# The gated-delta inverse: 16x16 diagonal blocks gathered one to a partition and solved by forward substitution

## What is computed

```python
G = jnp.cumsum(g, axis=-1)
decay = jnp.exp(jnp.where(incl, G[..., :, None] - G[..., None, :], -jnp.inf))
kb = k * beta[..., None]
L = jnp.where(strict, jnp.einsum('bhncd,bhnsd->bhncs', kb, k) * decay, 0.0)
rhs = jnp.concatenate([v * beta[..., None], kb * jnp.exp(G)[..., None]], axis=-1)
sol = lax.linalg.triangular_solve(L + jnp.eye(CHUNK), rhs, left_side=True, lower=True)
u, w = sol[..., :dv], sol[..., dv:]
# then, chunk after chunk:
v_new = u_c - w_c @ S;  o_c = q_c @ S + a_c @ v_new;  S = S * gl_c + k_c^T @ v_new
```

## Time and profile before

| | us |
|---|---|
| median of three runs | 2791.84 |
| the profiled execution, its time | 2790.25 |
| the profiled execution, its span | 2788.5 |
| TensorE busy | 2584.4 (93%) |
| VectorE busy | 1761.7 (63%) |
| ScalarE busy | 1150.0 (41%) |
| share of TensorE in the chain that ended last | 82% |
| share of VectorE and ScalarE in it | 9% and 5% |

### The profile page before, as it was taken

The page is one execution under the profiler, slowest core; times in us unless marked ns, Lnnn a source line. Parts: engine busy times, 40 slices in busy tenths (PEclk is TensorE's granted clock), DMA queues, the critical chain, the costliest instruction groups (busy, mean ns, idle before and its releaser), DMA issues.

```text
span 2788.5 us, 48740 instructions
## 1 busy us (share of the span) xinstructions
PE 2584.4 (93%) x17978; PEld 2278.9 (82%) x17978; DVE 1761.7 (63%) x2936; ACT 1150.0 (41%) x1720; POOL 73.7 (3%) x149
## 2 busy tenths in 40 slices
PE   6995789999998999988999999899999999889998
PEld 4873568885457899968889999799988999688998
DVE  1767574447964786765476676665557667654765
ACT  3333332220024544462354554644546446624544
POOL 0000000001100000000110000000000000000000
PEclk8997899999999999999999999999999999999999
DMA  7460033225752366530056551365524655300563
GB/s 262 166 196 1 28 116 106 90 88 184 242 192 83 121 196 192 178 113 1 24 170 189 178 181 61 116 186 180 167 92 136 195 181 159 128 1 27 177 187 131
DMA packets 104988, 377.96 MB, mean 136 GB/s; under 512 B 11671, under 2 KB 12695, under 8 KB 104352
## 3 DMA queue, kind: packets, MB, share of 16 engines
q1 hardware_dynamic: 91296, 327.58, 36.7%
q0 software_dynamic: 12528, 47.62, 5.2%
q10 hardware_dynamic: 1040, 1.05, 0.1%
HBM read 375.15 MB, written 1.05 MB: 135 GB/s over the span
## 4 chain that ended last, share of the span: by engine, by line
PE 82%; DVE 9%; ACT 5%; issue 2%; DMA 1%; POOL 0%; DVEq 0%; ACTq 0%; SPq 0%; POOLq 0%
PE gb L474 19%; PE gb L475 19%; PE gb L476 19%; PE gb L588 5%; PE gb L1439 2%; DVE w_lo L433 2%; PE mb L1457 2%; PE gb L1455 2%; PE gb L521 1%; PE gb L523 1%; PE mb L1736 1%; PE gb L522 1%; PE mb L554 1%; PE gb L997 1%; PE gb L1717 1%
## 5 line engine op out<-in xcount | busy, mean ns | idle before, releaser
L474 PE MATMUL gb<-Xs,w_hi 128*128 128x256 f32 (+1 forms) x3552 | 1063.3, 299 | 25.7 <-DVE Xs L637 12.5
L475 PE MATMUL gb<-Xs,w_hi 128*128 128x256 f32 (+1 forms) x3552 | 1059.0, 298 | 0.0
L476 PE MATMUL gb<-Xs,w_lo 128*128 128x256 f32 (+1 forms) x3552 | 1058.8, 298 | 0.0
L427 ACT ACTIVATE w_hi<-raw 128x1024 fp32r<-128x1024 f32 x592 | 622.8, 1058 | 858.2 <-PE gb L476 786.8
L433 DVE TENSOR_TENSOR w_lo<-raw,w_hi 128x1024 fp32r<-128x1024 f32 x592 | 715.9, 1223 | 249.6 <-ACT w_hi L427 246.4
L474 PEld LDWEIGHTS gb<-Xs,w_hi 128*128 128x128 f32 x3552 | 672.1, 189 | 64.6 <-issue 23.2
L475 PEld LDWEIGHTS gb<-Xs,w_hi 128*128 128x128 f32 x3552 | 671.2, 189 | 27.9 <-issue 1.0
L476 PEld LDWEIGHTS gb<-Xs,w_lo 128*128 128x128 f32 x3552 | 670.8, 189 | 27.3
L476 PE MATMUL gb<-Fs,w_lo 128*128 128x256 f32 x880 | 243.8, 277 | 0.0
L474 PE MATMUL gb<-Fs,w_hi 128*128 128x256 f32 x880 | 243.8, 277 | 0.0
L475 PE MATMUL gb<-Fs,w_hi 128*128 128x256 f32 x880 | 243.8, 277 | 0.0
(11 more groups left out here) (334 smaller groups left out, 2939.3 us busy)
## 6 DMA issues: line engine op xcount, KB each, us to landing
raw<-in_up SPq DMA_DIRECT2D x264, 512.0 KB, 3.6
raw<-in_down SPq DMA_DIRECT2D x96, 512.0 KB, 3.6
R<-in_mod_later POOLq DMA_DIRECT2D x80, 512.0 KB, 4.0
raw<-in_gdn_in SPq DMA_DIRECT2D x64, 512.0 KB, 3.6
raw<-in_down SPq DMA_DIRECT2D x48, 384.0 KB, 4.0
raw<-in_hgrn_in SPq DMA_DIRECT2D x32, 512.0 KB, 4.1
raw<-in_ev_in SPq DMA_DIRECT2D x24, 512.0 KB, 4.5
raw<-in_gla_in SPq DMA_DIRECT2D x24, 512.0 KB, 4.0
```

The source lines that it names most:

```text
L427: nc.scalar.activation(w_hi[:, slot], raw[:, slot], ACT.Identity).then_inc(*hi_ready.inc())
L474: nc.tensor.matmul(to, w_hi[:, w_slot, k, :], x_hi, start=start, stop=False)
L475: nc.tensor.matmul(to, w_hi[:, w_slot, k, :], x_lo, start=False, stop=False)
L476: return nc.tensor.matmul(to, w_lo[:, w_slot, k, :], x_hi, start=False, stop=stop)
```

## The change

The first four of the seven levels (blocks up to 16) go. In their place the 128 diagonal blocks of 16x16 (8 blocks in each of 16 instances) are gathered one to a partition, inverted there, and put back:

- VectorE makes three small selection tables once, at the program's start (`dve_picks`).
- VectorE masks `low_T` to its diagonal blocks, four heads at a time, after heads 3 and 7 of the score loop.
- TensorE gathers: 16 products whose stationary operand is one column in 16 of the masked matrices, and whose moving operand is a 128x16 selection table. The result is 128 partitions x (16x16).
- VectorE solves: for row r = 1 to 15 one multiply of r x r elements and one sum over them, each waiting for the one before.
- Meanwhile TensorE transposes v and k as before, but ScalarE now scales all four tiles of a head, and TensorE's transposes wait for ScalarE alone.
- The 128 small inverses are spread out to full block rows by VectorE (one multiply of 2048 elements) and ScalarE (8 scaled copies of 256 elements), turned back by 16 transposes each, and copied by VectorE and ScalarE (four copies of 512 elements each) to `inv_T` and `inv`.
- The levels then run from level 4: 12 steps in place of 28.

```diff
@@ pe_gdn
+            act_a.due("pe")
+            pe.wait_ge(*mixed.due("pe", 4))
+            pe.wait_ge(*low_masked.due("pe", 2))
+            if i == 0:
+                pe.wait_ge(*picks_made.due("pe"))
+            for r in range(SUB):
+                last = nc.tensor.matmul(mb[:, 2, r * SUB:(r + 1) * SUB], sub_rows[:, :, r], pick_row[:, :], start=True, stop=True)
+            last.then_inc(*subs_out.inc())
             for h in range(HG):
...
                 if h >= 2:
-                    pe.wait_ge(*act_a.due("pe", 2 if h == 2 else 1))
-                    pe.wait_ge(*dve_a.due("pe"))
+                    pe.wait_ge(*tokens_kept.due("pe"))
...
+            pe.wait_ge(*tokens_kept.due("pe", 2))
+            pe.wait_ge(*spread_dve.due("pe"))
+            for r in range(SUB):
+                last = nc.tensor.transpose(score_banks[r // 4][:, (r % 4) * P:(r % 4 + 1) * P],
+                                           sub_rows_T[:, :, :, r].rearrange("p b c -> p (b c)"), ident[:, :])
+                if r % 4 == 3:
+                    last.then_inc(*inv_T_turned.inc())
+            pe.wait_ge(*spread_act.due("pe"))
+            for c in range(SUB):
+                last = nc.tensor.transpose(gb[:, c // 4, (c % 4) * P:(c % 4 + 1) * P],
+                                           sub_cols[:, c].rearrange("p b i -> p (b i)"), ident[:, :])
+                if c % 4 == 3:
+                    last.then_inc(*inv_turned.inc())
+            pe.wait_ge(*inv_made.due("pe", 4))
+            pe.wait_ge(*inv_T_made.due("pe", 4))
+            steps = [(l, g) for l in range(FIRST_LEVEL, LEVELS) for g in range(4)]
@@ act_gdn
+                nc.scalar.activation(k_dec[:, h, :], gb[:, 2 + h % 2, 0:P], ACT.Identity, scale=e_last[:, h:h + 1])
+                nc.scalar.activation(kb_g[:, h, :], gb[:, 2 + h % 2, P:2 * P], ACT.Identity, scale=beta_g[:, h:h + 1]).then_inc(*tokens_kept.inc())
+            act.wait_ge(*solved.due("act"))
+            for b in range(NSUB):
+                last = nc.scalar.activation(sub_cols[:, :, b, :], sub_inv, ACT.Identity, scale=pick_sub[:, b:b + 1])
+            last.then_inc(*spread_act.inc())
+            for g in range(4):
+                act.wait_ge(*inv_turned.due("act"))
+                nc.scalar.activation(X[:, :, T:2 * T].rearrange("p h (m c) -> p h m c", c=SUB)[:, :, :, 4 * g:4 * g + 4],
+                                     gb[:, g, :].rearrange("p (c h m) -> p h m c", c=4, h=HG), ACT.Identity).then_inc(*inv_made.inc())
@@ dve_gdn
+            nc.vector.memset(sub_inv, 0.0).then_inc(*dve_step.inc())
...
+            nc.vector.tensor_copy(Pflat[:, 10240:10496:SUB + 1], ones[:, 0:SUB]).then_inc(*dve_step.inc())
             for h in range(HG):
...
+                if h % 4 == 3:
+                    dve.wait_ge(*mixed.sent())
+                    quad = lambda z: z[:, h - 3:h + 1].rearrange("p h a t -> p (h a) t")
+                    nc.vector.tensor_tensor(quad(low_sub), quad(low_T), same_sub[:, :].unsqueeze(1).broadcast_to([P, 2 * 4, P]),
+                                            ALU.mult).then_inc(*low_masked.inc())
+            dve.wait_ge(*subs_out.due("dve"))
+            dve.wait_ge(*dve_step.sent())
+            low = mb[:, 2, 0:SUB * SUB].rearrange("p (i j) -> p i j", j=SUB)
+            for r in range(1, SUB):
+                terms = sub_prod[:, 0:r * r].rearrange("p (c j) -> p c j", j=r)
+                link(dve, nc.vector.tensor_tensor(terms, sub_inv[:, 0:r, 0:r], low[:, r:r + 1, 0:r].broadcast_to([P, r, r]), ALU.mult))
+                last = nc.vector.reduce_sum(sub_inv[:, 0:r, r], terms, AX_X)
+                if r < SUB - 1:
+                    link(dve, last)
+            last.then_inc(*solved.inc())
...
+            nc.vector.tensor_tensor(sub_rows_T.rearrange("p b c i -> p b (c i)"), flat.unsqueeze(1).broadcast_to([P, NSUB, SUB * SUB]),
+                                    pick_sub[:, :].unsqueeze(2).broadcast_to([P, NSUB, SUB * SUB]), ALU.mult).then_inc(*spread_dve.inc())
+            for g in range(4):
+                dve.wait_ge(*inv_T_turned.due("dve"))
+                nc.vector.tensor_copy(sub_rows[:, :, 4 * g:4 * g + 4], score_banks[g].rearrange("p (i m) -> p m i", i=4)).then_inc(*inv_T_made.inc())
```

More of the change, by code:

```diff
@@ L39 @@
 LEVELS = 7
+SUB = 16
+NSUB = P // SUB
+FIRST_LEVEL = 4
 MOD_TILES = 16
@@ L247, in build @@
         dve_a = signal("dve_a")
+        picks_made = signal("picks_made")
+        low_masked = signal("low_masked")
+        subs_out = signal("subs_out")
+        solved = signal("solved")
+        spread_dve = signal("spread_dve")
+        spread_act = signal("spread_act")
+        inv_turned = signal("inv_turned")
+        inv_T_turned = signal("inv_T_turned")
+        inv_made = signal("inv_made")
+        inv_T_made = signal("inv_T_made")
+        tokens_turned = signal("tokens_turned")
+        tokens_kept = signal("tokens_kept")
         inv_y = signal("inv_y")
@@ L1364, in build @@
         inv_T = inst(Pflat, 8192)
+        low_sub = inv_T
+        sub_rows = inv_T.rearrange("p h a (b i) -> p (h a b) i", i=SUB)
+        sub_inv = Pflat[:, 10240:10496].rearrange("p (c i) -> p c i", i=SUB)
+        sub_prod = Pflat[:, 10496:10752]
+        sub_rows_T = M[:, :, :].rearrange("p h t -> p (h t)").rearrange("p (b c i) -> p b c i", b=NSUB, i=SUB)
+        sub_cols = W[:, 0:4, :].rearrange("p a t -> p (a t)").rearrange("p (c b i) -> p c b i", b=NSUB, i=SUB)
         prod = [Pflat[:, 10240 + 512 * s:10752 + 512 * s] for s in range(2)]
@@ L1424, in pe_gdn @@
                         last = nc.tensor.transpose(gb[:, bank, t * P:(t + 1) * P], P2[:, c + h, t * P:(t + 1) * P], ident[:, :])
[L1425 to L1431, removed]
+                last.then_inc(*tokens_turned.inc())
+            pe.wait_ge(*tokens_kept.due("pe", 2))
[14 more added lines that the diff above has]
+            steps = [(l, g) for l in range(FIRST_LEVEL, LEVELS) for g in range(4)]
             def product(n):
                 l, g = steps[n]
-                if l:
+                if l > FIRST_LEVEL:
                     pe.wait_ge(*inv_done.due("pe"))
@@ L1539, in act_gdn @@
             pe_a.due("act")
+            act.wait_ge(*act_a.sent())
+            act.wait_ge(*mixed.due("act", HG))
             for h in range(HG):
-                act.wait_ge(*pe_a.due("act"))
-                if h == 0:
-                    act.wait_ge(*mixed.due("act", HG))
+                act.wait_ge(*tokens_turned.due("act"))
                 for t in range(TC):
-                    last = nc.scalar.activation(vb[:, h, t, :], gb[:, h % 2, t * P:(t + 1) * P], ACT.Identity, scale=beta[:, t, h:h + 1])
-                last.then_inc(*act_a.inc())
-            for n in range(4 * LEVELS):
+                    nc.scalar.activation(vb[:, h, t, :], gb[:, h % 2, t * P:(t + 1) * P], ACT.Identity, scale=beta[:, t, h:h + 1])
+                nc.scalar.activation(k_dec[:, h, :], gb[:, 2 + h % 2, 0:P], ACT.Identity, scale=e_last[:, h:h + 1])
[8 more added lines that the diff above has]
+                                     gb[:, g, :].rearrange("p (c h m) -> p h m c", c=4, h=HG), ACT.Identity).then_inc(*inv_made.inc())
+            for n in range(4 * (LEVELS - FIRST_LEVEL)):
                 act.wait_ge(*inv_y.due("act"))
@@ L1629, in dve_gdn @@
+            for l in range(FIRST_LEVEL, LEVELS):
                 for g in range(4):
-                    if l:
-                        dve.wait_ge(inv_done.sem, inv_base_dve[0] + 4 * (l - 1) + g + 1)
+                    if l > FIRST_LEVEL:
+                        dve.wait_ge(inv_done.sem, inv_base_dve[0] + 4 * (l - 1 - FIRST_LEVEL) + g + 1)
                     dve.wait_ge(*inv_z.due("dve"))
@@ L2060, in _ @@
                                     ALU.mult).then_inc(*lam_prod.inc())
+            dve_picks(dve)
             dve_mod(dve)
```

21 lines of the change are left out of this document (15 added, 6 removed).

## The result

| | us |
|---|---|
| changed kernel, median of four runs | 2761.51 (2760.56 to 2771.83) |
| kernel before, median of four runs | 2791.53 (2790.07 to 2804.28) |
| ratio after to before | 0.9891, interval 0.9854 to 0.9928 |
| forecast | 2731, range 2714 to 2756 |
| changed kernel, the profiled execution: time, span | 2762.44, 2760.4 |

The kernel became 30 us faster, half of what was forecast, and its time lies outside the range.

A forecast was written before the change was run, and what follows sets the result against it. The inverse was taken as bound by TensorE and on the path. Each mixer: 15.1 us added, 42.9 removed, 2.3 back at start-up, -30.1; both -60.2, from 2790.25 to 2730.0, so a 2731 us median, range 2714 to 2756.

The forecast's parts named there:

- What bounds the kernel, and the 16 steps removed: In each mixer's inverse, bound by TensorE and on the path: 16 steps at 2.68 us go, saving 42.9 us.
- Masks: VectorE's two masking multiplies after the scores: 2.64 us, net 2.2 after catching up; TensorE starts to gather at 2.3.
- Gather: TensorE's sixteen 16-column products before the solve: 3.5 to 6.6 us, taken as 3.5 from line 1386.
- upper bound of 6.6: TensorE's gathering products: 6.6 us if reading every 16th element costs 1.88 times, as in VectorE's masked copies.
- the first rival: Stride-16 stationary loads and copies reading PSUM across take 1.88 times: 5.6 us a mixer, 2742 us; chance 16 in 100.
- Solve, tokens, spreading: Between gathering and turning back: VectorE's solve 8.0 us, ScalarE's tokens 9.4, spreading 2.29 on VectorE and 3.3 on ScalarE.
- Turning back and start-up: Transposes before the levels, partly at low clock, end at 24.2 us; the levels' start-up then gives 2.3 us back.
- At nothing: Tables at program start, some 1.3 us in VectorE's idle time, and clearing with the diagonal, 0.4 us, cost nothing.
- the fourth rival: Gain returns as a wait for weights or the output projection's weight split: near 2790 us; chance 2 in 100.

## Why the prediction was wrong

By the changed kernel's trace, gdn0 and gdn1, step by step:

| step | forecast, us | gdn0 | gdn1 |
|---|---|---|---|
| last score multiply of before to the gather | 2.3 | 1.6 | 1.9 |
| gather to the solve | 3.7 | 7.1 | 7.1 |
| solve | 8.0 | 8.2 | 8.2 |
| solve's end to turning back | 2.5 | 2.5 | 2.5 |
| turning back to the first product of the levels | 7.7 | 6.4 | 7.3 |
| sum: start of the levels | 24.2 | 25.8 | 27.0 |
| levels | 30.0 | 29.9 | 30.2 |

The first row counts from where the last score multiply ended in the kernel before, 12.06 and 10.37 us behind the decay multiply. From the changed kernel's own last score multiply it is 1.4 us in both.

- *What bounds the kernel, and the 16 steps removed.* Right: the levels take 29.9 and 30.2 us with 12 steps.
- *Masks.* Right within a microsecond. VectorE caught up more than I gave it.
- *Gather.* The term was 3.5 us and the measurement is 7.1, above the upper bound of 6.6. I took line 1386 as the nearest row; the stride doubled it at the full clock, and the low clock would have doubled it as well. This second failed step cost 3.6 us in each mixer and was in part made up by the masks and the turning back. It is the mechanism of the first rival, at its place, but nowhere else: the sixteen turning transposes with the same stride ran 113 ns apart at the full clock, and the copies across PSUM took 0.69 us, no more than whole rows.
- *Solve, tokens, spreading.* Right, 8.2 against 8.0 us for the solve and 9.1 against 9.4 for the tokens. (The two rows give 1.09 ns an element and not 1.04, which leaves the sum at some 4 us.) The sums over short rows cost what one long sum of as many elements costs. That the solve is on the path in full was shown by running it twice.
- *Turning back and start-up.* Right in kind. In gdn0 the clock was partly back, and 1.3 us were gained on the forecast.
- *At nothing.* The four table instructions ran from 20.16 to 21.4 us, in VectorE's idle time, as written. But the step that made the forecast wrong is here: I priced the tables by their instructions alone. Their 608 bytes cost 31 us where nothing else was changed, and 28 us came back when they were moved (some 4 of them by the clock of the cores), more than every other error together. The sum had no term for where the operands lie, and no rival for it; the fourth rival looked for lost time in waits behind the core, while it was lost within the products themselves, ahead of the core too.

The core alone gained 28.7 and 27.4 us against 30.1 each. With the tables behind `Xs` the kernel measured 2735.78 us, 5 us from the forecast and inside its range. So the mechanism of the change was right, and nearly all of the miss is one unseen side effect of its allocation. That the cores then gained 31.2 and 29.4 us, so near to 30.1, is partly luck: the gather was 3.6 us over its term, and a clock that came back early in that execution made up for it.

Left open: why the place matters, and why with a period of 256 bytes, which tensor ahead it is relative to, what draws a stage to 113.3 or 117.8 ns, and why a product's strided stationary operand costs twice where a transpose's does not.

## What to carry to other kernels

- A tensor added in the middle of the allocation moves every operand behind it. Put new ones last, and where a kernel is bound by products, try a few paddings of the moving operand: here they make up to 2.2%, though none that was tried beat the old place.
- When a change gives half of what it should, compare the stages that it did not touch first. Count the records in equal windows at the same granted clock; the busy share and the mean duration showed nothing.
- A product with few columns need not be a short one: with 16 columns it took 112 ns a record, as much as the transposes of 128 columns (109 to 113), and 217 with a strided stationary operand. In a stage with gaps TensorE's clock makes the same instructions some 2 us longer or shorter from one execution to the next (65.1 and 67.2 us for a core here), so judge an edit of a microsecond by several profiles.

## What the runs showed of the hardware

- Products of a 128x128 stationary block and 256 columns in fp32r (the activations as the moving operand), back to back at the full clock, came 113.3, 116.7, 117.8 or 120.0 ns apart, by the place of the activations relative to what is allocated ahead of them, modulo 256 bytes. At one place two of these paces occur, by stage and by execution (113.3 and 117.8 at the old place, 116.7 and 117.8 with 96 or 608 bytes). Products of 512 columns came some 233 ns apart at the old place and 227 where those of 256 columns came 120.0 apart.
- A float32 product of 16 columns whose stationary operand has a stride of 16 elements comes every 217 ns a record at the granted clock of 1.00 and at 0.50 alike; a contiguous one every 112 and every 213. A transpose with the same stride comes every 113 at 1.00.
- The 7.1 us of 16-column products of gdn1's gather, back to back behind 2.6 us of idle time, ran at a granted clock of 0.50 from start to end and did not lift it. With contiguous operands and 4 us of 256-column products directly ahead, the gather ran at 1.00 throughout.
- VectorE's multiply of 1024 elements took 1.23 us with contiguous operands and 1.90 to 2.00 us reading every 16th element.
- A sum of 15 rows of 15 elements took 0.39 us, as a multiply of 225 elements did.
